# A streaming encoder layer on one core: prompt attention by pairs of heads with keys along the row and a row scan, its twelve steps alternating with the twelve conv column blocks

## The reference, cut to what matters

```python
def stick_breaking(q, k, v, q_pos, k_pos):
    z = jnp.einsum('bqhd,bkhd->bhqk', q.astype(jnp.float32), k.astype(jnp.float32)) * (HEAD_DIM ** -0.5)
    mask = k_pos[None, :] < q_pos[:, None]
    log_keep = jnp.where(mask, jax.nn.log_sigmoid(-z), 0.0)
    after = lax.cumsum(log_keep, axis=3, reverse=True) - log_keep
    a = jnp.where(mask, jnp.exp(jax.nn.log_sigmoid(z) + after), 0.0)
    return jnp.einsum('bhqk,bkhd->bqhd', a, v.astype(jnp.float32)).astype(v.dtype)

def short_conv(u, u_past, conv_w):
    t = u.shape[1]
    ext = jnp.concatenate([u_past.astype(u.dtype), u], axis=1)
    y = sum(conv_w[j] * ext[:, j:j + t, :] for j in range(CONV_K))
    return y, ext[:, -(CONV_K - 1):, :]

# merge: m = sigmoid(ga) * (attn @ w_attn_branch) + sigmoid(gb) * ((cb * conv_y) @ w_conv_branch)
```

## Time and profile before

| | us |
|---|---|
| median of 3 runs (965.77 to 969.74) | 965.96 |
| the profiled execution | 967.6 |
| its span, first to last instruction | 966.0 |
| PE busy / PEld / DVE / ACT / POOL, share of the span | 92% / 78% / 59% / 50% / 13% |

### The profile page before, as it was taken

One profiled execution on the slowest core, in us unless ns is written; L12 is line 12 of the kernel. 1 busy time (PEld: TensorE's weight loads), 2 busy tenths in 40 slices (PEclk: granted clock), 3 DMA queues, 4 the chain that ended last, 5 costly groups with the idle time before them and its releaser, 6 DMA issues.

```text
span 966.0 us, 14010 instructions
## 1 busy us (share of the span) xinstructions
PE 886.3 (92%) x4976; PEld 751.1 (78%) x4976; DVE 566.6 (59%) x729; ACT 484.6 (50%) x671; POOL 126.7 (13%) x229
## 2 busy tenths in 40 slices
PE   5999999999999999999999828999999999982898
PEld 4788999955588999999878626888888888872686
DVE  4567217444343443333534615999999999994752
ACT  5313321366446563222321415888888888883331
POOL 3444710022200000000000040000000000003400
PEclk9999999999999999999999968999999999996799
DMA  8024793000075564533200579899999999996311
GB/s 308 1 88 131 237 292 117 13 1 1 26 250 185 192 232 142 197 96 106 87 23 1 196 292 359 291 407 408 410 409 410 409 409 410 409 372 202 115 44 55
DMA packets 118333, 201.28 MB, mean 208 GB/s; under 512 B 6430, under 2 KB 43966, under 8 KB 117264
## 3 DMA queue, kind: packets, MB, share of 16 engines
q1 hardware_dynamic: 109648, 170.58, 48.8%
q0 software_dynamic: 8640, 30.09, 9.0%
HBM read 173.34 MB, written 27.30 MB: 208 GB/s over the span
## 4 chain that ended last, share of the span: by engine, by line
PE 86%; DVE 5%; DMA 3%; ACT 2%; POOL 2%; issue 2%; SPq 0%; POOLq 0%; DVEq 0%; ACTq 0%
PE bank L421 25%; PE bank L423 24%; PE bank L422 24%; PE bank L1811 2%; PE bank L1657 2%; PE bank L1768 2%; PE bank L1798 2%; PE bank L1975 1%; PE bank L1868 1%; DVE wlo L391 1%; PE bank L1802 1%; POOL moe_rows L734 1%; DMA x<-in_x_prompt 1%; PE bank L1841 1%; DVE eo L1126 1%
## 5 line engine op out<-in xcount | busy, mean ns | idle before, releaser
L391 DVE TENSOR_TENSOR wlo<-raw,whi 128x1024 fp32r<-128x1024 f32 (+1 forms) x266 | 313.5, 1190 | 141.4 <-ACT whi L387 130.4
L387 ACT ACTIVATE whi<-raw 128x1024 fp32r<-128x1024 f32 (+1 forms) x266 | 274.4, 1034 | 187.3 <-PE bank L423 175.9
L421 PE MATMUL bank<-hh,whi 128*128 128x320 f32 x448 | 140.2, 313 | 0.0
L422 PE MATMUL bank<-hh,wlo 128*128 128x320 f32 x448 | 138.9, 310 | 0.0
L423 PE MATMUL bank<-hl,whi 128*128 128x320 f32 x448 | 138.8, 310 | 0.0
L421 PE MATMUL bank<-whi,hh 128*128 128x512 f32 x280 | 114.6, 409 | 9.2 <-DVE hl L1126 7.0
L423 PE MATMUL bank<-wlo,hh 128*128 128x512 f32 x280 | 111.4, 398 | 0.0
L422 PE MATMUL bank<-whi,hl 128*128 128x512 f32 x280 | 111.3, 398 | 0.0
L421 PE MATMUL bank<-whi,xh 128*128 128x512 f32 x256 | 103.1, 403 | 5.6 <-DVE xl L1126 5.6
L423 PE MATMUL bank<-wlo,xh 128*128 128x512 f32 x256 | 101.5, 397 | 0.0
L422 PE MATMUL bank<-whi,xl 128*128 128x512 f32 x256 | 101.3, 396 | 0.0
(11 more groups left out here) (262 smaller groups left out, 1261.6 us busy)
## 6 DMA issues: line engine op xcount, KB each, us to landing
raw<-in_w_exp_gate SPq DMA_DIRECT2D x64, 512.0 KB, 9.8
raw<-in_w_exp_up SPq DMA_DIRECT2D x64, 512.0 KB, 10.8
raw<-in_w_exp_down SPq DMA_DIRECT2D x64, 512.0 KB, 10.4
raw<-in_w_in SPq DMA_DIRECT2D x40, 512.0 KB, 6.3
moe_rows<-zero POOLq DMA_DIRECT2D x16, 512.0 KB, 13.2
ktc<-in_cache_kT SPq DMA_DIRECT2D x8, 1024.0 KB, 7.1
vc<-in_cache_v SPq DMA_DIRECT2D x8, 1024.0 KB, 5.5
xe<-moe_rows SPq DMA_DIRECT2D x16, 512.0 KB, 10.1
```

Source lines behind the costliest of these rows:

```text
L387: nc.scalar.activation(part(whi[:, u.slot], short), part(raws[u.raw], short), ACT.Copy).then_inc(s_hi, 1)
L391: nc.vector.tensor_tensor(out=part(wlo[:, u.slot], short), in0=part(raws[u.raw], short), in1=part(whi[:, u.slot], short).bitcast(F32), op= ...
L421: pe.matmul(out, a_hi, b_hi, start=first, stop=False, skip_group_check=True)
L422: pe.matmul(out, a_lo, b_hi, start=False, stop=False, skip_group_check=True)
```

## The change

Attention of the prompt is done in 12 steps, three for each pair of heads: query tile 3 against 4 key tiles; query tiles 2 and 0 against 3 and 1; query tile 1 against 2. Both heads of the pair stand side by side, so a step is 2 x 512, 2 x 512 or 2 x 256 wide. Queries are on the partitions and keys along the row, so the sum over later keys is a reversed row scan on DVE (`log_weights`), and the products with `um` and `neg` go. The weights must then be transposed by PE (`turn`), copied out by ACT (`turned_out`), and multiplied with v by key tile (`values`). One instruction per step takes the place of three per head on ACT and DVE, and of four masks on POOL.

Step k stands between the two halves of conv column block k on PE; ACT and DVE interleave likewise. The samples' part is one sample deeper: the gate block of sample 0 starts during the last steps, and `weights_turned` and `sample_values` of sample b - 1 stand in the period of sample b. On POOL the zero writes to `moe_rows` come after the last mask and the store of `ncv`. On SP `cache_k(0)` waits for the conv results instead of the last head.

```diff
+        gate_bank, branch_bank = bank[4:6], bank[6:8]
+
+        STEPS = 3 * HP
+        q_tiles = (((3, 0),), ((2, 0), (0, 3 * P)), ((1, 0),))
+        step_width = (W, W, 2 * P)
+        new_diagonal = ((3 * P, W), (2 * P, W), (P, 2 * P))
+
+        def scores_of(k):
+
+            first = 2 * (k % 2)
+            return zz[:, first:first + 2, 0:step_width[k % 3]]
+
+        def stick_of(k):
+            return stick[k % 3][:, :, 0:step_width[k % 3]]
...
+            sp.wait_ge(s_free, F_D)
+            cache_k(0)
             sp.wait_ge(s_vout, 16 * NT)
-            sp.wait_ge(s_hn, NT)
-            sp.wait_ge(s_av, H)
-            cache_k(0)
+            sp.wait_ge(s_av, STEPS)
             cache_v(0)
             for b in range(B):
...
-            with pool.Fori(0, NE) as e:
-                pool.dma_start(Xd[bass.ds(e * C, C), :].rearrange("r (a b) -> r a b", b=P),
-                               zero[:, None, :].to_broadcast([P, D // P, P])).then_inc(s_zero, 16)
...
+            for k in range(STEPS + 1):
+                if k:
+                    mask(k - 1, s_ea, s_am)
+                if k < STEPS:
+                    mask(k, s_spr, s_sp)
+                if k == 2 * KW + 1:
+                    last_inputs()
+
+            pool.wait_ge(s_trf, G_CONV + 1)
+            pool.dma_start(O[4].rearrange("o b j c -> (o b j) c"), ncv[0:2]).then_inc(s_ncvo, 16)
+            pool.dma_start(O[7].rearrange("o b j c -> (o b j) c"), ncv[2:]).then_inc(s_ncvo, 16)
+            with pool.Fori(0, NE) as e:
+                pool.dma_start(Xd[bass.ds(e * C, C), :].rearrange("r (a b) -> r a b", b=P),
+                               zero[:, None, :].to_broadcast([P, D // P, P])).then_inc(s_zero, 16)
...
+            def log_terms(k):
+                if k >= 3:
+                    act.wait_ge(s_pt, 2 * k - 4)
+                act.wait_ge(s_z, k + 1)
+                sc.activation(stick_of(k), scores_of(k), ACT.Abs).then_inc(s_ln1, 1)
+                act.wait_ge(s_ln1, 3 * k + 1)
+                sc.activation(stick_of(k), stick_of(k), ACT.Exp, scale=-1.0).then_inc(s_ln1, 1)
+                act.wait_ge(s_ln1, 3 * k + 2)
+                sc.activation(stick_of(k), stick_of(k), ACT.Ln, bias=1.0).then_inc(s_ln1, 1)
+
+            def exp_weights(k):
+                act.wait_ge(s_acc, k + 1)
+                sc.activation(stick_of(k), stick_of(k), ACT.Exp).then_inc(s_ea, 1)
+
+            def turned_out(k, e):
+                w = step_width[k % 3]
+                act.wait_ge(s_pt, 2 * k + e + 1)
+                if k:
+                    act.wait_ge(s_av, k)
+                sc.activation(turned[:, e, 0:w], bank[6][:, 0:w], ACT.Copy).then_inc(s_pto, 1)
+
+            def pair_hi(pair):
+                act.wait_ge(s_av, 3 * pair + 3)
+                sc.activation(ah[:, pair, 0:TP], bank[7][:, :], ACT.Copy).then_inc(s_ah, 1)
...
+            act.wait_ge(s_hn, NT)
+            sc.preload_act_table_set("natural_log_exp_and_others")
+            for k in range(STEPS):
+                if 0 < k <= KW:
+                    conv_out(k - 1, 1)
+                if k >= 5 and k % 3 == 2:
+                    pair_hi(k // 3 - 1)
+                if k >= 2:
+                    turned_out(k - 2, 0)
+                if k >= 1:
+                    exp_weights(k - 1)
+                log_terms(k)
+                if k >= 2:
+                    turned_out(k - 2, 1)
+                if k >= 1:
+                    split_hi(act, Unit(U_CC + k + 3), U_CC + k + 3 == U_C + 1)
+                if k < KW:
+                    conv_out(k, 0)
+
+            turned_out(STEPS - 2, 0)
+            exp_weights(STEPS - 1)
+            for j in range(KW - 1):
+                conv_hi(j)
+            turned_out(STEPS - 2, 1)
+            conv_hi(KW - 1)
+            split_hi(act, Unit(U_C + 3), True)
...
-                    new_key_weights()
-                weights(b)
                 gate(b, 0)
                 gate(b, 1)
-                weights_out(b)
+                if b:
+                    weights_out(b - 1)
+                    logs(b)
                 split_hi(act, gate_unit(b + 2))
+                weights(b)
                 split_hi(act, gate_unit(b + 2).plus(1), True)
...
+            def softplus_of(k):
+                dve.wait_ge(s_ln1, 3 * k + 3)
+                ve.scalar_tensor_tensor(out=stick_of(k), in0=scores_of(k), scalar=0.0, in1=stick_of(k), op0=ALU.max,
+                                        op1=ALU.add).then_inc(s_spr, 1)
+
+            def log_weights(k):
+                dve.wait_ge(s_sp, k + 1)
+                w = step_width[k % 3]
+                for e in range(2):
+                    for i, at_ in q_tiles[k % 3]:
+                        row_ = stick[k % 3][:, e, at_:at_ + (i + 1) * P]
+                        ins = ve.tensor_tensor_scan(out=row_[:, ::-1], data0=ones1[:, 0:1].to_broadcast([P, (i + 1) * P]),
+                                                    data1=row_[:, ::-1], initial=0.0, op0=ALU.mult, op1=ALU.add)
+                ins.then_inc(s_sum, 1)
+                dve.wait_ge(s_sum, k + 1)
+                tt(stick_of(k), scores_of(k), stick_of(k), ALU.subtract).then_inc(s_acc, 1)
+
+            def pair_lo(pair):
+                dve.wait_ge(s_ah, pair + 1)
+                tt(al[:, pair, 0:TP], bank[7][:, :], ah[:, pair, 0:TP].bitcast(F32), ALU.subtract).then_inc(s_al, 1)
...
+            for k in range(STEPS):
+                c, j = k // KW, k % KW
+                if k == KW:
+                    dve.wait_ge(s_free, F_CC + 2 * KW)
+                    dve.wait_ge(s_made, 12)
+                    dve.wait_ge(s_const, 16 * 9)
+                if KW < k <= 2 * KW:
+                    conv_in(k - 1 - KW, 1)
+                if 2 * KW < k:
+                    conv_gated(k - 1 - 2 * KW, 1)
+                if KW < k <= 2 * KW:
+                    dve.wait_ge(s_free, F_CC + 2 * k)
+                    conv(k - 1 - KW)
+                softplus_of(k)
+                if c == 1:
+                    conv_in(j, 0)
+                if c == 2:
+                    conv_gated(j, 0)
+                if k >= 1:
+                    split_lo(dve, Unit(U_CC + k + 3), U_CC + k + 3 == U_C + 1)
+                log_weights(k)
+                if k >= 5 and k % 3 == 2:
+                    pair_lo(k // 3 - 1)
+            conv_gated(KW - 1, 1)
+            split_lo(dve, Unit(U_C + 3), True)
...
-            place()
             new_keys_seen()
+            dve.wait_ge(s_tr, G_CONV + 1)
+            ve.tensor_copy(ncv[:, :], bank[0][0:2 + 2 * B, :]).then_inc(s_trf, 1)
             new_key_softplus()
+            new_key_weights()
+            new_key_rows()
+            dve.wait_ge(s_pt, 2 * STEPS)
+            dve.wait_ge(s_av, STEPS)
+            for j in range(KW):
+                conv_lo(j)
+            pair_lo(HP - 1)
             for b in range(B):
+                gated(b, 0, m[:, b, half_rows(0)])
+                if b:
+                    values_out(b - 1)
                 softplus(b)
-                if b == 0:
-                    new_key_weights()
-                    new_key_rows()
-                gated(b, 0, m[:, b, half_rows(0)])
-                values_out(b)
                 gated(b, 1, m[:, b, half_rows(1)])
-                keep(b)
+                if b:
+                    keep(b - 1)
                 split_lo(dve, gate_unit(b + 2))
                 split_lo(dve, gate_unit(b + 2).plus(1), True)
+            values_out(B - 1)
+            keep(B - 1)
             dve.wait_ge(s_ah, HP + 1)
             tt(al[:, :, TP:T], af[:, :, :], ah[:, :, TP:T].bitcast(F32), ALU.subtract).then_inc(s_al, 1)
...
+            def scores(k):
+                if k >= 2:
+                    pe.wait_ge(s_acc, k - 1)
+                pair = k // 3
+                z = scores_of(k)
+                for i, at_ in q_tiles[k % 3]:
+                    for e in range(2):
+                        r = slice(e * HD, (e + 1) * HD)
+                        ins = pe.matmul(z[:, e, at_:at_ + (i + 1) * P], qT[r, pair, i * P:(i + 1) * P],
+                                        kT[r, pair, 0:(i + 1) * P], start=True, stop=True, skip_group_check=True)
+                ins.then_inc(s_z, 1)
+
+            def turn(k, e):
+                if e == 0:
+                    pe.wait_ge(s_am, k + 1)
+                if k or e:
+                    pe.wait_ge(s_pto, 2 * k + e)
+                for n in range(step_width[k % 3] // P):
+                    ins = pe.transpose(bank[6][:, n * P:(n + 1) * P], stick[k % 3][:, e, n * P:(n + 1) * P], ident[:, :])
+                ins.then_inc(s_pt, 1)
+
+            def values(k):
+                pair = k // 3
+                pe.wait_ge(s_pto, 2 * k + 2)
+                if k % 3 == 0 and pair:
+                    pe.wait_ge(s_al, pair)
+                for i, at_ in q_tiles[k % 3]:
+                    for kb in range(i + 1):
+                        for e in range(2):
```

(102 more changed lines are left out.)

266 lines of the change are left out of this document (64 added, 202 removed).

## The result

The changed kernel takes **983.57 us** (median of 4 runs, 982.25 to 985.13) beside 967.83 us of the kernel before on the same chip: a ratio of 1.0164, 95% interval 1.0145 to 1.0183. It is slower by 1.6%; the forecast was 962 us with a range up to 973. The profiled execution has a span of 980.6 us, 14.6 us more than the 966.0 of before.

The account below looks back on a forecast made before the run. The ACT/DVE/POOL ring would pace attention at 30.6 us per pair. Despite a 20 us stall sample 1's period ends 7.6 us ahead; less 1.8, 0.6 and 1.5 leaves 3.7: 967.6 becomes 963.9, median 962 us, range 940 to 973.

Parts of the forecast that it names:

- S: Time at which PE begins the conv blocks, 109.5 us in the kernel before; the forecast's times count from it.
- PE's own work: PE in the attention steps: 29.3 us of sums removed, 8.8 us of transposes added, 27.9 us per pair, at worst 32.5.
- rival (b): Attention steps: scores and values do not overlap by head, 32.5 us per pair on PE, 969 us in all; chance 0.15.
- The loop between ACT, DVE and POOL: Attention steps: exp, logs, copy, splits, scans and subtraction wait on each other, 30.6 us per pair, setting the pace.
- the ring: The loop between ACT, DVE and POOL in the attention steps: 30.6 us per pair, more than PE's 27.9.
- The idle of 1 to 1.5 us before each step's values, my sign of being right: Attention steps: PE would wait 1 to 1.5 us at values, behind the second turned copy, if the forecast held.
- Rival (c): Handover from mask to scans: mask waits out the slot split, a step gains 1.2 us, 976 us in all; chance 0.15.
- log weights of step 11: End of the last attention step's log weights, forecast at S + 123, after first steps and three pairs of 30.6 us.
- The tail: Behind the last attention step: last values at S + 135.5, PE's branch block from near S + 141 to 144.5.
- The zero writes: From S + 132 they starve SP's load burst; `ktc` 1 lands near S + 172, stalling PE 20 us.
- Rival (a): SP's burst passes the zero writes, stall near 1.5 us, period 1 ends at S + 161, 944 us in all; chance 0.2.
- each period's slot load is now issued one period later and has no slack: Sample periods: the slot load's round takes 13.6 us against 13.7 of PE; 1.5 us lost in all.

## Why the prediction was wrong

The forecast would have the span at 962.3; it was 980.6, so 18.3 us are to be placed. S is 109.6 us in the trace of after.

1. **PE's own work** was taken too low. That two heads overlap held: per pair and at the full clock, scores 1.06 + 1.06 + 0.63, values 1.02 + 1.02 + 0.59 make 5.4 us against my 4.65, and far from the 9.3 without overlap, which ends rival (b). But with the transposes (2.4) and conv halves of 3.6 and 3.7 us instead of 3.5, a pair is 29.7 us on PE, not 27.9.

2. **The loop between ACT, DVE and POOL.** That the ring is longer than PE's work was wrong: it was 29.5 and 27.9, not 30.6, against PE's 29.7. The idle of 1 to 1.5 us before each step's values, my sign of being right, was nowhere; PE waited for `al` alone, at the borders of pairs. Rival (c) happened in one step. There the split began first and the mask, which takes 0.64 us elsewhere, took 1.57 and held up the scans by 0.54:

```profile
126.38 1.22 DVE L403 TENSOR_TENSOR wlo<-raw,whi 128x1024 fp32r<-128x1024 f32 x1
126.53 1.57 POOL L705 TENSOR_SCALAR_AFFINE_SELECT stick<-stick 128x512 f32<-128x512 f32 x1 [3.94 <-DVE stick L1282]
128.13 0.96 DVE L1291 TENSOR_TENSOR_SCAN stick<-ones,stick 128x384 f32<-128x384 f32 x1 [0.54 <-POOL stick L705]
```

In the other steps the mask came first, or ended before the split, as the prediction argued against (c), and took 0.41 to 0.64. What I left out was `al`. My list of a step's work on DVE did not hold it, and in the kernel before a pair had a bank of its own, so nobody on PE waited for it. Now PE's first values of a pair need the one bank 7 free, and the `al` that frees it stood behind the scans: 3.5 and 2.9 us in the steps, 2.0 in the tail, and the lower clock behind each. That the stage looks nearly right is luck, two errors of opposite sign: log weights of step 11 ended at 235.4, S + 125.8 against S + 123, and with `al` early it is S + 117. At the last values it is S + 141.7 against my S + 135.5, and with `al` early S + 128.8: the steps and their tail were priced 6.7 us too high, and `al`, with the lower clock behind it 12.9 us there, was not priced at all.

3. **The tail.** Last values end at 251.3, S + 141.7 against S + 135.5. 2.8 of the 6.2 us are the steps; `al` once more (0.6) and, at the lower clock, values of 1.52, a turn of 1.05 and six matmuls at 0.27 make 2.2; the rest is work in between that I had shorter. DVE's queue behind it (key rows, `cl`, `al`) was sized right: 5.1 us of wait.

4. **The zero writes**: mechanism and size right. First write at 248.7 instead of 241, since the `ncv` copy came later, yet `ktc` 1 landed 36.4 us after it (I had 40), at 285.1, S + 175.5 against S + 172. Rival (a) did not happen for this order of loads, but a part of it is true: the first load of a burst does pass, the later ones don't. Behind the stall the lower clock cost 2.9 us (scores 1.94 for 1.0, twelve matmuls at 0.27 for 0.15, values 1.64 for 1.27), not 1.5. Sample 1's period ended at 294.3, S + 184.7 against S + 179.6: 5.1 us of the miss up to here.

5. **The step that failed** is the 1.5 us for "each period's slot load is now issued one period later and has no slack". I counted one round, the slot's, at 13.6 us. The chain of after shows the other, longer one, for `ktc`:

```profile
307.19 0.37 SPq L487
...
307.60 0.51 SPq L386
...
308.15 0.58 SPq L386
...
308.78 9.14 DMA ktc<-in_cache_kT
...
317.96 1.06 PE zz L1841 x8
```

Values of sample b - 1, then `vc`, two slots and `ktc` on SP (1.6 us), 9.14 us to landing behind 1.75 MB of others, scores 1.06, a branch half 2.0, values 1.27: 15.1 us, where PE's work is 13.7. The loads were also dearer than their medians: `ktc` took 8.8 to 9.5 us, the gate slot 7.4 (8.2 at the last sample), where I took 7.0 and the earlier trace rows has 7.1 and 6.3. `ktc` now leaves 1.6 us behind `vc` instead of 3.1, which may be why; no run isolates that. From the end of sample 1's period to the scores of sample 7 there are five periods and a gate block, 68.6 + 7.4 = 76.0 us of work; it took 85.2. That is 9.2 us, and 5.5 more are what is left of the miss behind them, about the waits at the last sample (4.7 + 1.0). Less the 1.5 that I had: 13.2 us. With the 5.1 us of point 4 this is 18.3. The run with the loads ahead confirms it from the other side: its periods are 13.72 us and the wait of 4.7 us is gone. The 5.1 us up to there come from `al`, the term that the prediction put at nothing: with `al` early the scores of sample 1 start at 273.50 us instead of 285.15, and the kernel is ahead of the forecast at that point.

So the prediction knew the hazard, and named it, but closed it by one term with a median duration. Its own sum for the slot round left 0.1 us of slack; at such a distance the other loads of the same burst had to be laid out too.

## What to carry to other kernels

When work is moved one period later in a software pipeline, look at every wait in the queue that issues its loads. A load that stands behind a wait for the previous period's result turns prefetch into a loop, and the loop is to be summed with the burst's landing time, not with the median. One shared buffer (here bank 7) makes its release urgent: the instruction that frees it goes ahead of the long work of its engine. And where bulk writes can't be kept away from a burst of loads, the order within the burst decides: first what is wanted first.

## What the runs showed of the hardware

- Beside queued zero writes the first 1 MB load that SP issued took 8.5 us (12.1 in the other order) and later ones 15 to 31 us; without the writes the same burst lands in 5.5 to 8.7 us each. SP's own instruction for a 256 KB load took 7.89 us beside them (12.49 with the loads ahead), 0.58 without, and what SP had to issue next waited as long.
- A short wait costs more than itself: in the attention steps 8.4 us of PE's waits were 12.3 us of time, with the granted clock at 0.95 over such a pair and 1.00 without the wait; behind the long stall it was 0.57 for 7 us.
- Of a DVE instruction and a POOL mask that ran side by side, the later one stretched. The mask that began 0.15 us behind a slot split took 1.57 us instead of 0.64 (rows above). The same conv pass of DVE took 0.75 us alone, and 1.13 when a mask of 0.64 had begun 0.05 us before it (timelines of POOL and of DVE, after):

```profile
195.61 0.64 POOL L705 TENSOR_SCALAR_AFFINE_SELECT stick<-stick 128x512 f32<-128x512 f32 x1 [5.85 <-ACT stick L868]
```

```profile
195.66 1.13 DVE L1257 SCALAR_TENSOR_TENSOR yc<-up,convw,yc 128x512 f32<-128x512 f32 x1
```
